# Input turned as landed with its root applied later, gate rows scaled ahead, and both residuals turned by VectorE through shuffled transfers

## The chip, the core and the metric

The kernel runs on one core of one Trainium2 chip. The metric is the device time of one execution in microseconds. The core has five engines with instruction streams of their own that wait for one another on semaphores: TensorE (PE) multiplies, VectorE (DVE) and ScalarE (ACT) work elementwise, GpSimd (POOL) makes masks and issues transfers, and SyncE (SP) issues the weight transfers. Sixteen DMA engines carry every transfer, whichever engine issued it.

## What is computed

One decoder block over 16 meta tokens and 256 tokens, width 2048, all in float32. The reference, cut to what matters here:

```python
h = jnp.concatenate([meta, x], axis=1)              # 272 tokens
u = rmsnorm(h, attn_norm_w[l])                      # x * rsqrt(mean(x*x)) * w
z = u @ w_in[l]
hq, hf, hi, hg, aq, ak, av, iq, ik, iw, ga, gb = split_cols(z, IN_SIZES)
y_h = hgrn2_mix(hq, hf, hi, hg, lbs[l], hgrn_norm_w[l])
y_a = dsa_mix(aq, ak, av, iq, rmsnorm(ik, idx_k_norm_w[l]), iw, topk)
m = (jax.nn.sigmoid(ga) * (y_h @ w_branch_hgrn[l])
     + jax.nn.sigmoid(gb) * (y_a @ w_branch_dsa[l]))
h = h + m @ w_out[l]                                # first residual
u = rmsnorm(h, ffn_norm_w[l])
a = causal_dwconv(u @ w_ffn_gate[l], ffn_conv_w[l], ffn_conv_b[l])
h = h + (jax.nn.silu(a) * (u @ w_ffn_up[l])) @ w_ffn_down[l]   # second residual
return rmsnorm(h, final_norm_w)[:, N_META:]
```

## The kernel before

**Tiling.** Channels lie on the 128 partitions and tokens along the free dimension, so an input of 2048 channels is 16 blocks `k`. The work is cut into units: one unit is 128 output channels. For precision each float32 operand is split in a high and a low part (fp32r), and a unit is 16 steps of three products, high x high, low x high, high x low: 48 products of 128x128 weights with 258 columns (the 256 tokens and two meta tokens), accumulated in one PSUM bank. `u_hi`, `u_lo` hold the normalized input, `w_hi`, `w_lo` the weights of a unit, four buffers each.

**Stages.** 2 key units (done as one), 8 query, 24 recurrence, 32 gate, 24 attention, 8 output-gate, 16 merge, 16 output (`U_OUT`), then twice 44 feed-forward and 22 down units. The recurrence and the attention themselves run as jobs between products.

**Feeding.** SyncE loads weight panels of two units (2 MB) in two slots `raw`, each after `lo_ready` says that the slot's last unit has been split. ScalarE rounds a unit (`w_hi <- raw`, L1057) three units ahead and VectorE makes the rest (`w_lo`, L1358); `ahead(n)` does that for unit n+3. `projected` counts the units TensorE has finished.

**Start.** `x_tok` holds the meta rows and two halves of x with tokens on partitions. ScalarE sums squares (L1104, L1109), VectorE takes the root and scales `x_tok` (L1376, L1390); TensorE then turns three 128x128 pieces for each k (L673), ScalarE rounds them with the norm weight (L1127, `u_hi`), VectorE makes the rest (L1401, `u_lo`), and the key products (L652 to L654) and the first query unit follow. 36 products of ones (`warm_up`, L638) fill TensorE's time until then. After eight steps of unit 3 stands `key_squares` (L686).

**Gates.** The 32 gate units are spilled to DRAM: ScalarE copies the bank to `gate_st` and issues the transfer (L1231). In the merge stage GpSimd fetches a pair of gate rows into one of four buffers (L571) when `m_ready` says that the buffer is free; ScalarE applies the sigmoid (L1283).

**Output stage.** GpSimd fetches x again in panels (`x_st`, L577, L578). TensorE turns three pieces of it into the bank (L952) and accumulates the unit's 48 products on top (L960 to L962); banks 6 and 7 alternate, and unit n waits for `out_free`, the copy of unit n-2. VectorE copies the bank to `h_res` (L1691), ScalarE rounds it (L1296, `u2_hi`, shown as `u_hi`), VectorE makes the rest (L1693), both split a weight unit, GpSimd adds the squares (L583, L588), whose sum over channels TensorE makes within the first feed-forward unit (L979, L981).

**Down stage.** Tokens on partitions. TensorE turns `h_res` back into each bank before its first product (`residual`, L1000, four pieces to a bank, eight banks), and VectorE copies the bank to `h_tok` (L1748) in the first half; in the second half it adds.

The order in every engine is the order of the code; nothing is scheduled by a planner. The loops of the output stage are hardware loops (`Fori`).

## Time and profile before

| | |
|---|---|
| median of 3 runs | 1605.2 us (1605.15 to 1605.24) |
| profiled execution, its own time | 1604.96 us |
| its span | 1603.3 us |
| TensorE busy | 1590.7 us, 99% |
| VectorE busy | 961.1 us, 60% |
| ScalarE busy | 708.9 us, 44% |
| GpSimd busy | 91.9 us, 6% |
| moved by DMA | 290.36 MB, 181 GB/s |

The profile is one execution; times in it are counted from the span's start. In its rows PE is TensorE, DVE VectorE, ACT ScalarE, POOL GpSimd, SP SyncE; a q behind the name is that engine's own sequencer, where transfers are issued. L952 is line 952 of the kernel before. `out<-in` names what is written and read. Matmuls are pipelined, so the duration of one is longer than the distance to the next.

### The profile page before, as it was taken

Reading aid. Unit: us, or ns where it says so; the run is one execution under the profiler, and the core shown is the slowest. Engines: PE = TensorE matmul, PEld = TensorE weight load, DVE = VectorE, ACT = ScalarE, POOL = GpSimd, SP = SyncE. Lnnn points to the kernel's source line nnn. Section 1 sums busy time; section 2 is a strip of 40 time slices with the busy share of each in tenths; the row PEclk is TensorE's granted clock in tenths of the full one; section 3 lists DMA queues with packets and bytes.
Section 4 is the critical chain, followed back from the end, with each engine's and each line's share of the span. In section 5 each row is a group of like instructions: output and inputs, shape, how many; then the busy total and the mean of one; then the engine's idle time right before and its main releaser. Section 6 shows DMA issues by size and latency. Waiting matters only on the chain.

```text
span 1603.3 us, 29430 instructions
## 1 busy us (share of the span) xinstructions
PE 1590.7 (99%) x12222; PEld 1533.2 (96%) x12222; DVE 961.1 (60%) x1117; ACT 708.9 (44%) x741; POOL 91.9 (6%) x149
## 2 busy tenths in 40 slices
PE   9999999999999999999999999999999999999998
PEld 8999999999999999999999999999889999999886
DVE  7555778853355566766566666665445666666453
ACT  6333554544443345754435455544333334334342
POOL 1100050000000001111320000000000000000000
PEclk9999999999999999999999999999999999999999
DMA  7655565555555553577556565645455656565551
GB/s 236 207 158 166 162 200 178 179 178 178 178 162 185 183 158 106 176 231 239 182 170 203 164 198 169 201 165 191 178 206 172 198 171 195 166 200 193 200 209 54
DMA packets 244966, 290.36 MB, mean 181 GB/s; under 512 B 5665, under 2 KB 231186, under 8 KB 244498
## 3 DMA queue, kind: packets, MB, share of 16 engines
q1 hardware_dynamic: 238114, 278.78, 53.4%
q0 software_dynamic: 2176, 6.34, 1.2%
q10 hardware_dynamic: 4608, 4.23, 0.8%
q8 instruction: 55, 0.90, 0.2%
q14 instruction: 13, 0.11, 0.0%
HBM read 283.02 MB, written 6.32 MB: 180 GB/s over the span
## 4 chain that ended last, share of the span: by engine, by line
PE 98%; DVE 1%; ACT 0%; DMA 0%; issue 0%; SPq 0%; DVEq 0%; ACTq 0%
PE ps L616 25%; PE ps L617 24%; PE ps L618 24%; PE ps L1016 5%; PE ps L1015 5%; PE ps L1013 5%; PE ps L962 2%; PE ps L960 2%; PE ps L961 2%; PE ps L738 1%; PE ps L713 0%; PE ps L855 0%; PE ps L952 0%; DMA x_tok<-in_x_dram 0%; PE ps L748 0%; PE ps L1000 0%
## 5 line engine op out<-in xcount | busy, mean ns | idle before, releaser
L616 PE MATMUL ps<-u_hi,w_hi 128*128 128x258 f32 (+2 forms) x2944 | 841.0, 286 | 0.0
L617 PE MATMUL ps<-u_lo,w_hi 128*128 128x258 f32 (+2 forms) x2944 | 833.6, 283 | 0.0
L618 PE MATMUL ps<-u_hi,w_lo 128*128 128x258 f32 (+2 forms) x2944 | 833.2, 283 | 0.0
L1358 DVE TENSOR_TENSOR w_lo<-raw,w_hi 128x2048 fp32r<-128x2048 f32 x259 | 595.6, 2300 | 358.4 <-ACT w_hi L1057 358.1
L1057 ACT ACTIVATE w_hi<-raw 128x2048 fp32r<-128x2048 f32 x259 | 496.1, 1916 | 573.9 <-PE ps L618 411.5
L616 PEld LDWEIGHTS ps<-u_hi,w_hi 128*128 128x128 f32 x2944 | 555.5, 189 | 5.1 <-DVE z_qf L1458 2.5
L617 PEld LDWEIGHTS ps<-u_lo,w_hi 128*128 128x128 f32 x2944 | 555.4, 189 | 0.3
L618 PEld LDWEIGHTS ps<-u_hi,w_lo 128*128 128x128 f32 x2944 | 555.2, 189 | 0.0
L1013 PE MATMUL ps<-w_hi,hid_hi 128*128 128x512 f32 x352 | 137.7, 391 | 0.0
L1016 PE MATMUL ps<-w_lo,hid_hi 128*128 128x512 f32 x352 | 137.0, 389 | 0.0
L1015 PE MATMUL ps<-w_hi,hid_lo 128*128 128x512 f32 x352 | 137.0, 389 | 0.0
L1016 PEld LDWEIGHTS ps<-w_lo,hid_hi 128*128 128x128 f32 x352 | 66.1, 188 | 13.8
L1015 PEld LDWEIGHTS ps<-w_hi,hid_lo 128*128 128x128 f32 x352 | 66.1, 188 | 13.5
L1013 PEld LDWEIGHTS ps<-w_hi,hid_hi 128*128 128x128 f32 x352 | 66.1, 188 | 13.4
L960 PE MATMUL ps<-m_hi,w_hi 128*128 128x258 f32 x256 | 73.7, 288 | 0.0
L962 PE MATMUL ps<-m_hi,w_lo 128*128 128x258 f32 x256 | 72.6, 284 | 0.0
L961 PE MATMUL ps<-m_lo,w_hi 128*128 128x258 f32 x256 | 72.2, 282 | 0.0
L1229 ACT ACTIVATE gate_st<-ps 128x258 f32<-128x258 f32 x32 | 12.4, 387 | 100.0 <-PE ps L618 100.0
L961 PEld LDWEIGHTS ps<-m_lo,w_hi 128*128 128x128 f32 x256 | 48.6, 190 | 0.0
L960 PEld LDWEIGHTS ps<-m_hi,w_hi 128*128 128x128 f32 x256 | 48.4, 189 | 0.0
L962 PEld LDWEIGHTS ps<-m_hi,w_lo 128*128 128x128 f32 x256 | 48.3, 189 | 0.0
L1731 DVE TENSOR_TENSOR g_raw<-ps,h_rs 128x258 f32<-128x258 f32 x44 | 18.8, 427 | 39.6 <-PE ps L618 37.9
(288 smaller groups left out, 1280.0 us busy)
## 6 DMA issues: line engine op xcount, KB each, us to landing
raw<-in_w_in_dram SPq DMA_DIRECT2D x48, 2048.0 KB, 8.4
raw<-in_w_ffn_gate_dram SPq DMA_DIRECT2D x22, 2048.0 KB, 8.0
raw<-in_w_ffn_up_dram SPq DMA_DIRECT2D x22, 2048.0 KB, 8.0
raw<-in_w_ffn_down_dram SPq DMA_DIRECT2D x20, 2048.0 KB, 7.7
raw<-in_w_out_dram SPq DMA_DIRECT2D x8, 2048.0 KB, 8.9
raw<-in_w_branch_hgrn_dram SPq DMA_DIRECT2D x8, 1024.0 KB, 5.4
raw<-in_w_branch_dsa_dram SPq DMA_DIRECT2D x8, 1024.0 KB, 8.5
gate_spill<-gate_st ACTq DMA_DIRECT2D x32, 129.0 KB, 3.8
```

Of the source, the lines that this page charges most:

```text
L616: mm(acc, w_hi[s][:, k, :], mov_hi(k), start=(k == first), stop=False)
L617: mm(acc, w_hi[s][:, k, :], mov_lo(k), start=False, stop=False)
L618: ins = mm(acc, w_lo[s][:, k, :], mov_hi(k), start=False, stop=(k == last))
L960: mm(acc, w_hi[n % 4][:, k, :], m_hi[:, k, :], start=False, stop=False, skip_group_check=True)
L961: mm(acc, w_hi[n % 4][:, k, :], m_lo[:, k, :], start=False, stop=False, skip_group_check=True)
L962: ins = mm(acc, w_lo[n % 4][:, k, :], m_hi[:, k, :], start=False, stop=(k == KT - 1), skip_group_check=True)
L1013: mm(acc, hid_hi[:, f, rows], down_hi[s][:, i, :], start=(f == 0 and half == 1), stop=False, skip_group_check=True)
L1015: mm(acc, hid_lo[:, f, rows], down_hi[s][:, i, :], start=False, stop=False, skip_group_check=True)
L1016: ins = mm(acc, hid_hi[:, f, rows], down_lo[s][:, i, :], start=False, stop=(f == FH - 1), skip_group_check=True)
L1057: activation(w_hi[m % 4][:], raw[(m // 2) % 2][:, :, P * (m % 2):P * (m % 2) + P], ACT.Copy)\
L1358: v.tensor_tensor(w_lo[m % 4][:], raw[(m // 2) % 2][:, :, P * (m % 2):P * (m % 2) + P], w_hi[m % 4][:].bitcast(F32), ALU.subtract).then_in ...
L1731: link(v.tensor_tensor(g[:], ps[4 * half + u][:, 0:TQ], h_rs[:], ALU.mult))
```

## The change

The input: x is turned by TensorE as it lands, without its root. The meta rows come first (16 pieces), then seven blocks of the first 128 tokens, seven more, then the second 128 tokens. `u_hi` and `u_lo` hold x times the norm weight. The roots are computed beside the first units, spread over the partitions by one product of ones with a diagonal (`x_rs`), and every eviction of a unit multiplies by `x_rs`. The gate rows are spilled unscaled; GpSimd multiplies each fetched pair by `x_rs` (`scale_gates`). Warm-up products: 5 where there were 36. The key and first query panels are loaded in halves.

The first residual: GpSimd fetches x in four groups of sixteen transfers (`x_quad`), each 32 partitions x 8 x 32 elements, so that 32x32 blocks lie where a VectorE transpose of blocks gives the full transpose. VectorE turns them (`xt`, and `xm` for the meta rows) and adds them to the bank.

The second residual: VectorE turns each `h_res` by blocks into one of four `h_sh`, ScalarE issues four transfers that write it shuffled to DRAM (`h_spill`), GpSimd loads all of it to `h_tok` after the stage, and VectorE adds the banks to it.

```diff
+        x_blocks = x[0].rearrange("(b j) (k a i) -> a j k b i", j=32, a=4, i=32)
+        meta_blocks = meta_tokens.rearrange("j (k a i) -> a j k i", a=4, i=32)
+        h_blocks = h_spill.rearrange("(b j) (k a i) -> a j k b i", j=32, a=4, i=32)
...
+
+        def x_part(n):
+
+            if n <= EARLY:
+                return n - 1, x_bank(n - 1)[:, 0:P], slice(META, END)
+            if n <= 2 * EARLY:
+                return n - EARLY - 1, x_bank(n - EARLY - 1)[:, 2 * P:3 * P], slice(END, T)
+            return n - EARLY - 1, x_bank(n - EARLY - 1)[:, 0:2 * P], slice(META, T)
...
+            def scale_gates(slot, count):
+                pool.wait_ge(gate_in[slot], count)
+                pool.tensor_tensor(gates[slot][:], gates[slot][:],
+                                   x_rs[:, T0:T].rearrange("p (a t) -> p a t", a=1).to_broadcast([P, 2, TQ]), ALU.mult)\
+                    .then_inc(gate_scaled, 1)
...
+                    scale_gates((a + 3) % 4, 16 * i + (16 if a == 0 else 32))
...
+            def x_quad(q):
+                for a in range(4):
+                    for k in range(4):
+                        pool.dma_start(x_sh[q % 2][32 * a:32 * a + 32, k, :].rearrange("j (b i) -> j b i", i=32),
+                                       x_blocks[a, :, 4 * q + k, :, :]).then_inc(x_sh_in[q % 2], 16)
...
-            for b in range(2):
-                steps.link(pool, pool.memset(x_st[b][:, 0, :], 0.0))
-                x_panel(b, slice(256 * b, 256 * b + 256))
...
+            pool.wait_ge(projected, U_MERGE)
+            pool.wait_ge(ya_ready, 9)
+            pool.memset(xm_sh[:], 0.0).then_inc(xm_zeroed, 1)
+            x_quad(0)
+            pool.wait_ge(xm_zeroed, 1)
+            for a in range(4):
+                pool.dma_start(xm_sh[32 * a:32 * a + 2, :, :], meta_blocks[a, T0:META, :, :]).then_inc(xm_in, 16)
+            pool.wait_ge(projected, U_OUT)
+            x_quad(1)
+            for n in range(16):
+                if n in (4, 8):
+                    pool.wait_ge(xt_turned, n)
+                    x_quad(n // 4 + 1)
...
+            for c in range(2):
+                pool.dma_start(h_tok[c][:], h_spill[:, 1024 * c:1024 * c + 1024].rearrange("(t p) n -> p t n", p=P))\
+                    .then_inc(h_in, 16)
...
-            warm_up(14)
+            warm_up(3)
...
+            def turn(out, t, k):
+                return nc.tensor.transpose(out, x_tok[t][:, P * k:P * k + P], ident[:])
+
+            pe.wait_ge(meta_zeroed, 1)
+            pe.wait_ge(x_in[0], 16)
+            for b in range(4):
+                for k in range(4):
+                    ins = turn(ps[b][:, P * k:P * k + P], 0, 4 * b + k)
+                ins.then_inc(meta_turned, 1)
+            pe.wait_ge(norm_ready, 1)
+            pe.wait_ge(x_in[1], 16)
+            for k in range(EARLY):
+                if k >= 3:
+                    pe.wait_ge(meta_weighted, k - 2)
+                turn(x_bank(k)[:, 0:P], 1, k).then_inc(x_turned, 1)
+            for k in range(EARLY, 2 * EARLY):
+                pe.wait_ge(ul_ready, k - EARLY + 1)
+                turn(x_bank(k)[:, 0:P], 1, k)
+            pe.wait_ge(x_in[2], 16)
+            for k in range(EARLY):
+                turn(x_bank(k)[:, 2 * P:3 * P], 2, k).then_inc(x_turned, 1)
+
...
+            def turn_rest(k):
+
+                pe.wait_ge(ul_ready, k + 1)
+                if k >= 2 * EARLY:
+                    turn(x_bank(k)[:, 0:P], 1, k)
+                turn(x_bank(k)[:, P:2 * P], 2, k).then_inc(x_turned, 1)
...
+            pe.wait_ge(key_hi, 1)
+            for k in range(8):
+                keys_high(k)
+                if k + 11 < KT:
+                    turn_rest(k + 11)
+                if k == 1:
+                    pe.wait_ge(key_lo, 1)
+                    keys_low(0)
+                if k >= 1:
+                    keys_low(k)
+            pe.wait_ge(hi_ready, 2)
+            for k in range(8, KT):
+                keys_high(k)
+            pe.wait_ge(lo_ready, 2)
+            for k in range(8, KT):
...
+            def spread_roots():
+                pe.wait_ge(x_diag, 3)
+                mm(ps[2][:, 0:T], ones[:], diag[:, P - META:3 * P], start=True, stop=True).then_inc(x_spread, 1)
...
-                    bank = ps[6 + u % 2]
-                    for t in range(3):
-                        ins = mm(bank[:, P * t:P * t + P], x_st[u // 2][:, t, P * (u % 2):P * (u % 2) + P], ident[:],
-                                 is_transpose=True, start=(t == 0), stop=False, skip_group_check=True)
-                    ins.then_inc(xt_turned, 1)
...
+                        ins = products(ps[6 + u % 2][:, 0:TQ], n % 4, (k,), lambda k: m_hi[:, k, :],
+                                       lambda k: m_lo[:, k, :])
...
-                        if f == 0 and half == 0:
-                            residual(c, j % 2, t)
...
+            def round_x(n):
+
+                k, part, toks = x_part(n)
+                act.wait_ge(x_turned, n)
+                activation(u_hi[:, k, toks], part, ACT.Copy, scale=vec_a[:, V_ATTN + k:V_ATTN + k + 1])\
+                    .then_inc(uh_ready, 1)
+
+            def round_keys(half):
+
+                activation(w_hi[0][:, half, 0:KEYS], raw[0][:, half, 0:KEYS], ACT.Copy)\
...
+                round_x(n)
+            act.wait_ge(meta_weighted, 4)
+            activation(u_hi[:, :, 0:META], u_meta[:], ACT.Copy).then_inc(meta_rounded, 1)
+            for n in range(EARLY + 1, KT + EARLY + 1):
+                if n == 2 * EARLY:
+                    act.wait_ge(key_in, 16)
+                    round_keys(slice(0, 8))
+                if n == 2 * EARLY + 2:
+                    act.wait_ge(landed[0], landed_by[0])
+                    round_keys(slice(8, KT))
+                if n == KT + EARLY:
+                    act.wait_ge(query_in, 16)
+                    activation(w_hi[2][:, 0:8, :], raw[1][:, 0:8, 0:P], ACT.Copy).then_inc(hi_half, 1)
+                round_x(n)
+            act.wait_ge(landed[1], landed_by[1])
+            activation(w_hi[2][:, 8:KT, :], raw[1][:, 8:KT, 0:P], ACT.Copy).then_inc(hi_ready, 1)
+            round_unit(3, 3, landed_by[1])
+            activation(junk[:], x_tok[1][:], ACT.Square, accum_out=rstat[:, 1:2]).then_inc(x_sum, 1)
             act.wait_ge(x_sum, 3)
-            act.wait_ge(x_part, 2)
-            activation(rstat[:, 5:6], rstat[:, 2:3], ACT.Sqrt, bias=rstat[:, 7:8], scale=1.0 / D).then_inc(x_std, 1)
...
+            for u in range(16):
+                act.wait_ge(out_free, u + 3)
+                activation(u2_hi[:, u, :], h_res[:, u, :], ACT.Copy, scale=vec_a[:, V_FFN + u:V_FFN + u + 1])\
+                    .then_inc(u2h_ready, 1)
+                ahead(U_OUT + u + 1)
+                act.wait_ge(h_turned, u + 1)
+                for a in range(4):
+                    act.dma_start(h_blocks[a, :, u, :, :],
+                                  h_sh[u % 4][32 * a:32 * a + 32, :].rearrange("j (b i) -> j b i", i=32))\
+                        .then_inc(h_out[u % 4], 16)
             act.wait_ge(ssq_sum, 1)
...
+            def rest_x(n):
+
+                k, part, toks = x_part(n)
+                dve.wait_ge(uh_ready, n)
+                v.scalar_tensor_tensor(u_lo[:, k, toks], part, vec_a[:, V_ATTN + k:V_ATTN + k + 1],
+                                       u_hi[:, k, toks].bitcast(F32), ALU.mult, ALU.subtract).then_inc(ul_ready, 1)
+
...
+            dve.wait_ge(x_std, 1)
+            v.reciprocal(rstat[:, 0:3], rstat[:, 3:6]).then_inc(x_rstd, 1)
+            dve.wait_ge(x_rstd, 1)
+            for t in range(3):
+                v.tensor_scalar(diag[:, P * t:P * t + P], ident[:], rstat[:, t:t + 1], None, ALU.mult).then_inc(x_diag, 1)
+            dve.wait_ge(x_spread, 1)
+            v.tensor_copy(x_rs[:], ps[2][:, 0:T]).then_inc(x_rs_ready, 1)
+            dve.wait_ge(x_rs_ready, 1)
             dve.wait_ge(projected, 2)
-            v.tensor_copy(k_raw[0:KEYS, :], ps[1][0:KEYS, 0:T]).then_inc(z_free, 2)
...
-                v.tensor_copy(z_g[:, h, :], ps[m % 2][:, 0:TQ]).then_inc(z_free, 1)
+                v.tensor_tensor(z_g[:, h, :], ps[m % 2][:, 0:TQ], x_rs[:, T0:T], ALU.mult).then_inc(z_free, 1)
...
+            for u in range(16):
+                m, h = U_OUT + u, h_res[:, u, :]
+                if u == 0:
+                    dve.wait_ge(xm_in, 64)
+                    v.transpose(xm[:].rearrange("p k t -> p (k t)"), xm_sh[:].rearrange("p k t -> p (k t)"))\
+                        .then_inc(xm_turned, 1)
+                    dve.wait_ge(xm_turned, 1)
+                if u % 4 == 0:
+                    dve.wait_ge(x_sh_in[(u // 4) % 2], 256 * (u // 8) + 256)
+                v.transpose(xt[u % 2][:], x_sh[(u // 4) % 2][:, u % 4, :]).then_inc(xt_turned, 1)
+                dve.wait_ge(xt_turned, u + 1)
+                dve.wait_ge(projected, m + 1)
+                v.tensor_tensor(h[:, 0:2], ps[6 + u % 2][:, 0:2], xm[:, u, 0:2], ALU.add)
+                v.tensor_tensor(h[:, 2:TQ], ps[6 + u % 2][:, 2:TQ], xt[u % 2][:], ALU.add).then_inc(out_free, 1)
+                dve.wait_ge(u2h_ready, u + 1)
+                v.scalar_tensor_tensor(u2_lo[:, u, :], h, vec_a[:, V_FFN + u:V_FFN + u + 1], u2_hi[:, u, :].bitcast(F32),
+                                       ALU.mult, ALU.subtract).then_inc(u2l_ready, 1)
+                ahead(m + 1, m + 1)
+                if u >= 4:
+                    dve.wait_ge(h_out[u % 4], 64 * (u // 4))
+                v.transpose(h_sh[u % 4][:], h[:, 2:TQ]).then_inc(h_turned, 1)
...
-                    if half == 0:
-                        v.tensor_copy(h, bank).then_inc(down_added, 1)
-                    else:
-                        v.tensor_tensor(h, bank, h, ALU.add).then_inc(down_added, 1)
+                    v.tensor_tensor(h, bank, h, ALU.add).then_inc(down_added, 1)
```

The order of the instructions, at two places. Output stage, ScalarE; before, inside its loop:

```order
L1296 ACTIVATE u_hi<-h_res,vec_a 128x258
L1054 REGISTER_ALU
L1056 ISA
L1057 ACTIVATE w_hi_53<-raw_50 128x2048
L1295 REGISTER_ALU
L1296 ISA x2
L1296 ACTIVATE u_hi<-h_res,vec_a 128x258
L1054 REGISTER_ALU
L1057 ACTIVATE w_hi_54<-raw_50 128x2048
```

and now:

```order
L1391 ACTIVATE u_hi<-h_res,vec_a 128x258
L1142 ACTIVATE w_hi_54<-raw_50 128x2048
L1396 DMA h_spill<-h_sh_134 32x8x32 x4
L1391 ACTIVATE u_hi<-h_res,vec_a 128x258
L1142 ACTIVATE w_hi_51<-raw_49 128x2048
L1396 DMA h_spill<-h_sh_135 32x8x32 x4
```

Between the weights of one unit and the next rounding of h now stand four issues, which wait for VectorE's `h_sh`. The same stage on VectorE (L1691 is the copy, L1693 and L1812 the rest of u2, L1358 and L1455 the rest of a weight unit); before:

```order
L1691 COPY h_res<-ps 128x258
L1692 REGISTER_ALU
L1693 ISA
L1693 SCALAR_TENSOR_TENSOR u_lo<-h_res,vec_a,u_hi 128x258
L1357 REGISTER_ALU
L1358 TENSOR_TENSOR w_lo_57<-raw_50,w_hi_53 128x2048
```

and now:

```order
L1806 STREAM_TRANSPOSE xt_129<-x_sh_128 128x256
L1809 TENSOR_TENSOR h_res<-ps,xm 128x2
L1810 TENSOR_TENSOR h_res<-ps,xt_129 128x256
L1812 SCALAR_TENSOR_TENSOR u_lo<-h_res,vec_a,u_hi 128x258
L1455 TENSOR_TENSOR w_lo_57<-raw_50,w_hi_53 128x2048
L1817 STREAM_TRANSPOSE h_sh_133<-h_res 128x256
```

A block transpose of x stands ahead of the add, and one of h behind the weights. GpSimd, at the passage from merge to output; before:

```order
L591 MEMSET ssq 128x258
L593 MEMSET x_st_124 128x256
L577 DMA x_st_124<-in_x_dram 128x2x256
L578 DMA x_st_124<-in_meta_tokens_dram 2x256
L593 MEMSET x_st_125 128x256
```

and now:

```order
L608 TENSOR_TENSOR gates_125<-gates_125,x_rs 128x516
L645 MEMSET ssq 128x258
L648 MEMSET xm_sh 128x512
L631 DMA x_sh_127<-in_x_dram 32x8x32 x16
L652 DMA xm_sh<-in_meta_tokens_dram 2x16x32 x4
L631 DMA x_sh_128<-in_x_dram 32x8x32 x16
```

The last gate pair is scaled first, and 20 issues stand ahead of the first add where there were two.

## Rows read from the trace of the kernel before

**Rows 1.** The page's first part: busy us, share of the span, instructions.

```profile
PE 1590.7 (99%) x12222; PEld 1533.2 (96%) x12222; DVE 961.1 (60%) x1117; ACT 708.9 (44%) x741; POOL 91.9 (6%) x149
```

**Rows 2.** TensorE's waits: who for whom, total us, times, longest.

```profile
PE ps L616 <- DVE gates L1673: 0.9, 1, 0.9
```

**Rows 3.** Chain in order of time: start us, us, what; output stage, sums, down stage.

```profile
755.73 0.33 PE ps L952 x3
...
767.94 0.33 PE ps L952 x3
...
850.61 0.43 PE ps L981 x2
...
1100.30 0.43 PE ps L1000 x4
```

**Rows 4.** TensorE's timeline in unit 3: start us, us, instruction.

```profile
36.44 0.72 PE L686 MATMUL ps<-k_sq,ones 64*128 64x272 f32 x2
```

**Rows 5.** Timeline of the start: start us, us, instruction, [idle before, releaser].

```profile
1.91 6.17 PE L638 MATMUL ps<-ones 128*128 128x128 f32 x28 [1.91 <-POOL bias L484]
...
6.90 1.92 ACT L1104 ACTIVATE junk<-x_tok 128x2048 f32<-128x2048 f32 x1 [0.27 <-DMA x_tok<-in_x_dram]
...
8.16 4.29 PE L638 MATMUL ps<-ones 128*128 128x128 f32 x36
...
13.62 2.38 ACT L1127 ACTIVATE u_hi<-ps,vec_a 128x272 fp32r<-128x272 f32 x6 [0.26 <-PE ps L673]
```

**Rows 6.** Timelines of VectorE and ScalarE in one output unit, together.

```profile
780.30 0.43 DVE L1691 COPY h_res<-ps 128x258 f32 x1 [0.79 <-PE ps L962]
780.95 0.51 ACT L1296 ACTIVATE u_hi<-h_res,vec_a  x1 [3.77 <-DVE h_res L1691]
781.37 1.90 ACT L1057 ACTIVATE w_hi<-raw 128x2048 fp32r<-128x2048 f32 x1
...
783.30 2.66 DVE L1358 TENSOR_TENSOR w_lo<-raw,w_hi 128x2048 fp32r<-128x2048 f32 x1 [1.18 <-ACT w_hi L1057]
```

**Rows 7.** VectorE's timeline: the key normalization, then a merge unit.

```profile
38.66 1.84 DVE L1431 RECIPROCAL k_rs<-k_rs 128x272 f32<-128x272 f32 x1
...
41.67 0.28 DVE L1436 MEMSET score<- 128x272 f32 x1
...
728.65 2.29 DVE L1358 TENSOR_TENSOR w_lo<-raw,w_hi 128x2048 fp32r<-128x2048 f32 x1 [0.73 <-ACT w_hi L1057]
730.86 0.42 DVE L1681 TENSOR_TENSOR m_lo<-gates,m_hi 128x258 f32 x1
```

**Rows 8.** GpSimd's groups by form: instruction, count, busy us, mean ns.

```profile
L583 POOL TENSOR_TENSOR h_sq<-h_res 128x258 f32 x12 | 7.5, 623 | 19.3 <-DVE h_res L1691 19.2
L577 POOL DMA_DIRECT2D x_st<-in_x_dram x8 | 6.2, 769 | 45.5 <-PE ps L952 44.9 <-POOL x_st L593 0.6
```

**Rows 9.** GpSimd's timeline at the last gate request.

```profile
731.94 0.72 POOL L571 DMA_DIRECT2D gates<-gate_spill  x1 [4.95 <-DVE m_lo L1681]
```

**Rows 10.** ScalarE's timeline in the gate stage.

```profile
388.24 0.34 ACTq L1231 DMA_DIRECT2D gate_spill<-gate_st  x1
388.63 1.92 ACT L1057 ACTIVATE w_hi<-raw 128x2048 fp32r<-128x2048 f32 x1 [0.41 <-ACT gate_st L1229]
```

**Rows 11.** Transfers: KB each, median us from issue to landing (672 to 740, whole).

```profile
gates<-gate_spill POOLq DMA_DIRECT2D x12, 258.0 KB, 5.4
...
x_st<-in_meta_tokens_dram POOLq DMA_DIRECT2D x8, 2.0 KB, 5.9
```

**Rows 12.** Stage row, 745 to 834: PE busy, granted clock, DMA share, GB/s.

```profile
745.00:834.00 89.00, 89.00 (x746) 1.00 0.61 197
```

**Rows 13.** DMA: packets in 9 to 10 us; queue q10 in 300 to 340.

```profile
DMA packets 975, 0.31 MB, mean 312 GB/s; under 512 B 975, under 2 KB 975, under 8 KB 975
...
q10 hardware_dynamic: 864, 0.79, 5.9%
```

**Rows 14.** Stage row, 1.9 to 3 us: busy, clock (third from the end), DMA.

```profile
1.90:3.00 1.10, 1.09 (x5) 1.09 (x6) 1.10 (x1) 1.06 (x1) 0.00 (x0) 1.00 0.72 164
```

More of the change, by code:

```diff
@@ L42 @@
 KEYS = 64 + IDXH
-LEFT = 1280
+EARLY = 7
 U_KI = 0
@@ L1719, in _ @@
                         if u == 3:
+                            if half == 0:
+                                for r in range(4):
+                                    dve.wait_ge(h_out[r], 4 * 64)
                             low(0)
```

315 lines of the change are left out of this document (141 added, 174 removed).

## The prediction

> **What bounds the kernel now.** I read the page first: TensorE is busy for 99% of the span, VectorE for 60, ScalarE for 44 [rows 1]. What TensorE executes is therefore the time, apart from its waits, and the list of its waits holds, beside the wait for the first constants, nothing longer than 0.9 us [rows 2]. A change can gain by taking work from TensorE or by letting its steady run begin earlier, and it loses where it makes a feeding engine slower than TensorE. The averages of VectorE and ScalarE don't tell that, so I then read the timelines of the two stages where the change loads them, the start and the output projection. All sums are in the clock of the profiled execution (span 1603.3, time 1604.96 us); the median of the three runs is 0.24 above it.
>
> **TensorE's pace.** Two output units last 12.21 us (755.73 to 767.94), of which two groups of three transposes are 0.66 [rows 3]. So a unit of 48 products is 5.78 us, 0.12 a product.
>
> **Start: the roots out of the way.** Before, squares, roots and the scaling of x stand between its landing and its transposes. The first product of key_squares stands after eight of the sixteen steps of unit 3, at 36.44 [rows 4]; 24 products earlier, at 33.55, unit 3 began.
> After, x is turned as it lands: tokens 0 to 127 at 6.9 [rows 5], 16 meta transposes before. Then ScalarE sets the pace. Six roundings of 272 columns take 2.38, 0.40 each [rows 5]; 2048 weights take 1.90 [rows 6]. From these I take 0.28 for 128 columns, 0.39 for 256, 0.65 for half the key weights, 1.05 for half a query unit. First turned block at 8.0; seven roundings to 10.0; the meta one to 10.4; TensorE's next transposes let the eighth begin at 10.75; six to 12.4; key weights to 13.1; two to 13.75; key weights to 14.4; seven to 17.15; query weights to 18.2; the last to 18.6; VectorE's rest of it to 19.1. TensorE then has two high products and eight low ones left: 20.3. Unit 2: 16 high products to 22.2, eight low ones to 23.2, a wait until VectorE has made the second half of its low weights (19.1 + 1.2 + 2.2 for a sum of squares over 2048 columns + 1.2 = 23.7), 24 more to 26.6. The product that spreads the roots adds two fp32 records like L686, about 0.65. **Net 33.55 - 26.6 - 0.65 = -6.3 us.** By the same steps units 4 to 7 have their low weights 2 to 4 us before TensorE comes. The evictions become products with x_rs; for 258 columns a copy out of PSUM takes 0.43 and a product of two operands 0.42 [rows 6, 7], so they cost nothing, and the roots lie in VectorE's free time.
> **Gates.** GpSimd scales each pair after it lands: 516 columns, twice an h_sq of 0.62 [rows 8], 1.25 us in a unit of 5.78 in which it had one issue of 0.72 [rows 9]. A pair is asked for four units before it is used and needs some 7 of those 23 us. Nothing, then; uncovered it would be 1.25 a unit, 20 us.
>
> **Transposes that leave TensorE.** The order shows all 48 with x_st and all 32 with h_res gone. 16 x 0.33 = **-5.3 us**, if TensorE isn't made to wait, and 8 groups of four at 0.43 = **-3.5 us** [rows 3]; for the latter VectorE adds where it copied, far ahead of need.
>
> **What the output stage gets instead.** VectorE's row for a unit is: turn x, add (h is made), rest of u2, rest of a weight unit, turn h. ScalarE's is: round u2, round a weight unit, wait until h is turned, issue four transfers, and only then the next unit. That closes a loop: h(u) turned, four issues, u2_hi(u+1), w_hi, w_lo, h(u+1) turned. Its length: hand-over 0.2 (copy ends 780.73, ScalarE starts 780.95); four issues of 0.34 [rows 10] with 0.04 between, 1.5; u2_hi to the start of w_hi 0.42; w_hi 1.90 and hand-over 0.03 [rows 6]; w_lo 2.21 until the next operation starts [rows 7]; and the 32x32 transpose of 256 columns, which this trace doesn't have. Around it stand a memset of 272 columns (0.28), a product of 258 (0.42) and, far off, a reciprocal of 272 (1.84) [rows 7]. I take 0.40, as an operation that passes each column once, and keep 0.28 to 0.6 for the range (at 1.84 the loop would cost 20 us more). Sum **6.66 us against TensorE's 5.78**. Before, ScalarE idled 3.77 us ahead of each u2_hi [rows 6]. Bounds of the loop: 6.35 (hand-over 0.1, issues 1.36, transpose 0.28) and 7.3 (issues 1.7, w_lo 2.6 as beside GpSimd [rows 6], transpose 0.6). add(u) frees the bank of unit u+2, so TensorE can run one unit ahead of it and no more.
> When does the loop start? GpSimd issues x_sh behind the gates. The last gate request is at 731.94 [rows 9] and lands after some 5.4 [rows 11]: 737.3; scaling 1.25 and two memsets: 739.5; 16 issues at 0.78 [rows 8] to 752.0; four shorter ones for the meta rows, which I put at 0.55, the last at 753.6; landing 5.9 later [rows 11]: 759.5. VectorE turns both (0.7 + 0.4) and adds: add(0) ends at A0 = 761.3. Output unit 0 starts at 749.6 (6.1 before the row at 755.73 [rows 3]), so TensorE ends unit 1 at 749.6 + 2 x 5.78 = 761.2 and wants that bank then: the slack is gone at the first unit. A1 = A0 + 6.1, A2 = A0 + 12.8, A15 = A2 + 13 x 6.66 = **860.7**; the square of unit 15 (0.2 + 0.62) and its product (0.1 + 0.43) end at 862.0. Before, that product, L981, ended at 851.04 [rows 3]. The stage is **+11.0 us** longer where it should be 5.3 shorter: the loop costs 16.3. Weights don't run out, since w_lo of unit u+4 is ready 5 us after add(u), two loops before TensorE wants it; after the stage all catch up.
> **Sum:** -6.3 + 11.0 - 3.5 = +1.2; 1606.2 for the profiled execution, **1606.4** by the median.
>
> **Rivals.** (A) *The loop doesn't bind*: the issues run beside ScalarE's activations and x_sh is there in time. Then -6.3 - 5.3 - 3.5 = -15.1: **1590.1**. For it: TensorE's work really goes. Against: in the gate stage the next activation starts at 388.63, after the issue of 388.24 to 388.58, not beside it [rows 10].
> (B) *Short packets fill the DMA engines* (slower). x comes in and h goes out in pieces of 32 elements, 128 bytes: in two units 2048 reads and 2048 writes, 128 of each per engine. In this stage the engines are busy for 0.61 [rows 12], 7.4 of 12.2 us; a double loop of 13.3 leaves 5.9, so it decides from 5900 / 128 = 46 ns for a read and a write together. Key weights of 320 bytes came at 975 packets in 1 us, 16 ns on each of 16 engines; the gate spill's writes took 5.9% of 16 x 40 us for 864 packets, 44 ns [rows 13]. At 16 + 16 it is hidden; at 44 + 44 two units take 7.4 + 11.3 = 18.7 us, 2.7 more per unit, 38 in 14 units, less some 15 us by which the weights run ahead: +23, **1629**. I hold 16 for likelier, since those packets moved 312 GB/s, as fast as long ones.
> The Trainium skill, page DMA: Bandwidth & Descriptors, section Specifications, says that below 512 B an engine reads, modifies and writes. By that rule the writes of h would be the dear half and B likelier; the 320-byte rows of this trace are loads and don't decide it.
> (C) *Slow TensorE at the start.* 28 records of the ones-products took 6.17 us from 1.91, 36 took 4.29 from 8.16 [rows 5]: the first ran at half the rate, though the clock's row there says 1.00 [rows 14]. The change drops 31 of 36 such products. If the low rate lasts to 20 us, 45 key products take 0.12 more each, a part of it covered: about +4.5, **1610.9**.
> The Trainium skill, page TensorE: Matmul & The Clock Gate, Part 1, tells of 1.2 GHz until the array has been busy and 2.4 GHz then; that is C's mechanism.
>
> **How the numbers follow.** Forecast 0.62. Its own range: 14 loops of -0.3 to +0.65 are -4.3 to +9, the landing of x_sh 2 either way, the start 1: 1600 to 1617. A 0.11, B 0.15, C 0.12. A measurement of this kernel tells about 0.2%, 3.2 us. Faster than 1602.0: A and 0.12 of the forecast, 0.23. Within: 0.36 of the forecast and 0.01 of C, 0.37. Slower than 1608.4: B, 0.11 of C, 0.14 of the forecast, 0.40. The range 1600 to 1619 leaves out A and the far end of B, 0.19.
>
> **What would show it.** The last product of unit 2 near 26.6. In the output stage ScalarE's wait ahead of its issues ends with VectorE's h_sh, add(u) comes every 6.6 us, and TensorE waits for VectorE's h_res some 0.9 us a unit, 10 to 16 us in all. If TensorE's waits stay as short as now, A is right; if w_hi waits for a weight transfer, or h_sh for h_spill, B; if products before 20 us come at 0.24 us, C. I would be wrong above all if four issues cost ScalarE far from 1.5 us, or the shuffled transfers land far from 6 us after their issue.

## The result: 4 us slower

The changed kernel takes 1609.53 us, the median of 8 runs (1608.50 to 1612.13), against 1605.24 for the kernel before (1604.99 to 1605.32) on the same chip: ratio 1.0029, 95% interval 1.0019 to 1.0039. That is +4.3 us where +1.2 was forecast. The profiled execution took 1610.17 us (span 1608.6), 5.2 more than that of before. The forecast stands by its mechanism and is off in three sizes, of which one offset a part of the other two; the experiments below take them apart.

The page of the changed kernel, first part; it answers to [rows 1]:

```profile
PE 1581.4 (98%) x12082; PEld 1520.2 (95%) x12082; DVE 977.0 (61%) x1175; ACT 708.5 (44%) x746; POOL 148.0 (9%) x218
```

TensorE lost 9.3 us of work and the kernel became slower: TensorE now waits. Its waits from 740 to 870 us (who for whom, total us, times, longest); before, the longest wait after the start was the one of [rows 2], elsewhere:

```profile
PE ps L679 <- DVE h_res L1810: 11.4, 11, 1.4
PE ps L679 <- DVE u_lo L1812: 3.2, 1, 3.2
PE ps L1075 <- POOL h_sq L637: 0.4, 1, 0.4
```

The timeline of one output unit, VectorE and ScalarE together (start us, us, instruction, [idle before, releaser]); it answers to [rows 6]:

```profile
836.15 0.44 DVE L1817 STREAM_TRANSPOSE h_sh<-h_res 128x256 f32<-128x256 f32 x1
...
836.62 2.02 ACTq L1396 DMA_DIRECT2D h_spill<-h_sh  x4
...
838.70 0.51 ACT L1391 ACTIVATE u_hi<-h_res,vec_a 128x258 fp32r<-128x258 f32 x1 [4.78 <-issue]
839.11 1.90 ACT L1142 ACTIVATE w_hi<-raw 128x2048 fp32r<-128x2048 f32 x1
...
841.04 2.29 DVE L1455 TENSOR_TENSOR w_lo<-raw,w_hi 128x2048 fp32r<-128x2048 f32 x1 [1.32 <-ACT w_hi L1142]
843.25 0.44 DVE L1817 STREAM_TRANSPOSE h_sh<-h_res 128x256 f32<-128x256 f32 x1
```

This is the loop of the forecast, from one turned h to the next in 7.10 us: hand-over and issues 2.55, u2_hi 0.41, w_hi and hand-over 1.93, w_lo 2.21. ScalarE's idle time ahead of u2_hi, once a wait for the copy of h, now is "issue": of the 4.78 us its sequencer waits 2.70 for the turned h and is then busy for 2.02 with the four transfers. The adds of units 1 to 15 start at 759.04 and 858.15 us, 7.08 apart.

The start of the loop: GpSimd's issues, and VectorE's first operations of the stage.

```profile
735.27 9.28 POOL L631 DMA_DIRECT2D x_sh<-in_x_dram  x16
744.54 2.40 POOL L652 DMA_DIRECT2D xm_sh<-in_meta_tokens_dram  x4
...
751.85 0.71 DVE L1801 STREAM_TRANSPOSE xm<-xm_sh 128x512 f32<-128x512 f32 x1 [2.95 <-DMA xm_sh<-in_meta_tokens_dram]
752.60 0.45 DVE L1806 STREAM_TRANSPOSE xt<-x_sh 128x256 f32<-128x256 f32 x1
753.08 0.16 DVE L1809 TENSOR_TENSOR h_res<-ps,xm 128x2 f32<-128x2 f32 x1
753.16 0.41 DVE L1810 TENSOR_TENSOR h_res<-ps,xt 128x256 f32<-128x256 f32 x1
```

The first part of the kernel: TensorE's first transposes, ScalarE's first roundings, and the first scores, a landmark that both kernels have.

```profile
4.49 4.53 PE L710 MATMUL ps<-ident,x_tok 128*128 128x128 f32 x23 [0.72 <-DMA x_tok<-in_meta_tokens_dram]
...
8.45 1.92 ACT L1195 ACTIVATE u_hi<-ps,vec_a 128x128 fp32r<-128x128 f32 x7 [1.99 <-PE ps L710]
...
69.81 0.97 PE L817 MATMUL ps<-ki,iq_st 64*128 64x144 f32 x8
```

In the kernel before, the same scores (L713 there) stand at:

```profile
75.21 0.97 PE L713 MATMUL ps<-ki,iq_st 64*128 64x144 f32 x8
```

So the start gained 5.4 us, not 6.3. From here the account is simple: 5.4 us ahead, the product with h_sq (L1075) ends at 860.02 us against 851.04 before, 9.0 us behind, so the output stage cost 14.4; the end is 5.2 behind, so the down stage gave 3.8 back.

### The profile page after: what moved, and what is told of

Same layout as the page of the kernel before. It is cut to its first block, busy times and chain, and to the rows that moved or that the text cites. A ratio compares the mean times of both kernels' runs of the same rounds, so it can differ in the third digit from the quotient of the medians.

```text
span 1608.6 us, 29146 instructions
## 1 busy us (share of the span) xinstructions
PE 1581.4 (98%) x12082; PEld 1520.2 (95%) x12082; DVE 977.0 (61%) x1175; ACT 708.5 (44%) x746; POOL 148.0 (9%) x218
## 3 DMA queue, kind: packets, MB, share of 16 engines
q0 software_dynamic: 4000, 8.45, 1.9%
## 4 chain that ended last, share of the span: by engine, by line
PE 90%; issue 3%; ACT 2%; ACTq 2%; DVE 1%; POOL 1%; DMA 1%; SPq 0%; DVEq 0%; POOLq 0%
PE ps L679 24%; PE ps L680 23%; PE ps L681 23%; PE ps L1101 5%; PE ps L1098 5%; PE ps L1100 5%; ACT w_hi L1142 2%; ACTq L1396 2%; PE ps L842 1%; POOL x_sh L631 1%; PE ps L817 0%; DVE h_sh L1817 0%; PE ps L710 0%; PE ps L959 0%; DMA xm_sh<-in_meta_tokens_dram 0%
## 5 line engine op out<-in xcount | busy, mean ns | idle before, releaser
L1455 DVE TENSOR_TENSOR w_lo<-raw,w_hi 128x2048 fp32r<-128x2048 f32 x259 | 597.2, 2306 | 352.4 <-ACT w_hi L1142 352.0
L1098 PE MATMUL ps<-w_hi,hid_hi 128*128 128x512 f32 x352 | 136.9, 389 | 0.0
L679 PE MATMUL ps<-m_hi,w_hi 128*128 128x258 f32 x256 | 73.4, 287 | 11.4 <-DVE h_res L1810 11.4
L1098 PEld LDWEIGHTS ps<-w_hi,hid_hi 128*128 128x128 f32 x352 | 66.1, 188 | 13.6
L1391 ACT ACTIVATE u_hi<-h_res,vec_a 128x258 fp32r<-128x258 f32 x16 | 8.2, 512 | 78.9 <-issue 71.9
```

What stands on the lines that cost most here:

```text
L679: mm(acc, w_hi[s][:, k, :], mov_hi(k), start=(k == first), stop=False)
L1098: mm(acc, hid_hi[:, f, rows], down_hi[s][:, i, :], start=(f == 0), stop=False, skip_group_check=True)
L1455: v.tensor_tensor(w_lo[m % 4][:], raw[(m // 2) % 2][:, :, P * (m % 2):P * (m % 2) + P], w_hi[m % 4][:].bitcast(F32), ALU.subtract).then_in ...
```

## The experiments

All times are medians; every kernel was timed beside the kernel before, which took 1605.3 to 1605.4 us each time. Each is given as an edit to the changed kernel.

| kernel | us | against before |
| --- | --- | --- |
| start and gates alone | 1599.97 | 0.9967 (0.9954 to 0.9979) |
| and x turned by VectorE | 1594.13 | 0.9930 (0.9917 to 0.9944) |
| the change | 1609.53 | 1.0029 (1.0019 to 1.0039) |
| h turned ahead of w_lo | 1590.27 | 0.9905 (0.9890 to 0.9921) |
| issues behind the next rounding | 1594.09 | 0.9929 (0.9915 to 0.9942) |
| that, last two behind the root | 1594.47 | 0.9927 (0.9913 to 0.9941) |
| that of two rows up, x early | 1590.44 | 0.9907 (0.9892 to 0.9922) |
| the change, x early | 1608.17 | 1.0017 (1.0008 to 1.0026) |
| the change, eight issues | 1637.41 | 1.0198 (1.0182 to 1.0213) |
| h ahead of w_lo, ten warm-ups | 1591.55 | 0.9913 (0.9900 to 0.9927) |
| h ahead of w_lo, one warm-up | 1589.99 | 0.9903 (0.9888 to 0.9918) |
| that, x early | 1589.90 | 0.9904 (0.9887 to 0.9922) |

**The parts one by one.** First the start and the gates alone, with the output and down stages of before:

```
-                products(..., m_hi, m_lo)                # output unit without x
+                transpose(x_st) x3, products onto them   # as before
-                v.transpose(xt), two adds; v.transpose(h_sh); four issues; load of h_tok
+                v.tensor_copy(h, bank); residual(c, u, t) on TensorE, as before
```

> The change's first two parts alone: the new start and the gates scaled by GpSimd. The output stage and the down stage are those of before (x_st and h_res turned by TensorE, no transfers of h). Theory (the start gains what the trace of the changed kernel shows at L817, 75.28 - 69.88 = 5.4 us, nothing of it is lost before the end, and the gates cost nothing): 1605.2 - 5.4 = 1599.8 us, the output stage as long as before. Rival (part of the stage's +14.4 us comes from the first parts, for instance from weight loads that run at another distance, or the gates): 1602 us or more. The forecast's start term, -6.3, would give 1598.9.

It took 1599.97 us: -5.4. Its trace is 5.5 us ahead at the first scores (69.69 us) and 5.3 at the product with h_sq (845.16 against 850.44), so the gates cost some 0.2 us at most, and none of the first parts lengthens the output stage.

Then x turned by VectorE as in the change, but h turned by TensorE:

```
-                v.transpose(h_sh[u % 4][:], h[:, 2:TQ])
-                act.wait_ge(h_turned, u + 1); four act.dma_start(h_blocks..., h_sh...)
-            pool.dma_start(h_tok[c][:], h_spill...)
+                residual(c, j % 2, t)                    # in the down stage, as before
```

> The changed kernel with the first residual turned by VectorE, but the second by TensorE as before: no turned copy of h, no issues of its transfers on ScalarE, no load of h. Theory (the output stage was stretched by the loop through ScalarE's four issues; without them no loop is over TensorE's 5.78 us): the stage is TensorE's again and shorter than before by the 5.3 us of x_st, so 1605.2 - 5.4 (start) - 5.3 = 1594.5 us. Rival 1 (the turn of x and the two adds, with their transfers, stretch the stage by themselves): over 1600 us. Rival 2 (the late first add, which waits for the input's transfers, costs): 1596 to 1599 us.

1594.13 us, the first theory's 1594.5: taking x's transposes away is worth 5.8 us, and the turn of x, its two adds and the shuffled loads cost nothing. Whatever cost 15 us and more in the change stands in the lines taken out here.

**The loop, broken in two places.** The first kernel moves one operation of VectorE:

```
                 v.scalar_tensor_tensor(u2_lo[:, u, :], ...)
+                if u >= 4:
+                    dve.wait_ge(h_out[u % 4], 64 * (u // 4))
+                v.transpose(h_sh[u % 4][:], h[:, 2:TQ]).then_inc(h_turned, 1)
                 ahead(m + 1, m + 1)                      # w_lo
-                (the same three lines)
```

> The changed kernel with one step of VectorE moved: h(u) is turned ahead of the rests w_lo instead of behind them, all work and all transfers the same. Theory (the loop: ScalarE's issues wait for h turned, that waits for w_lo, that for w_hi, and the next u2_hi waits behind the issues): with the turn ahead of w_lo ScalarE has 0.42 + 1.93 + about 1.9 = 4.3 us of work a unit, under TensorE's 5.78; the output stage falls from 7.11 to 5.8 us a unit, about 20 us: 1589 to 1591 us. Rival 1 (the transfers of 128 bytes stretch the stage, by the DMA engines' time): 1603 to 1610, no better than the changed kernel. Rival 2 (ScalarE's issues take their time from its sequencer, whatever the order): about 1600.

1590.27 us: 19.3 us less than the change, with every instruction and every transfer kept. This is what the loop cost. Both rivals fall with it: transfers of 128 bytes and issues on ScalarE are all there, in a shorter stage. ScalarE's timeline in one unit of this kernel shows why:

```profile
826.10 1.90 ACT L1142 ACTIVATE w_hi<-raw 128x2048 fp32r<-128x2048 f32 x1
827.10 1.82 ACTq L1396 DMA_DIRECT2D h_spill<-h_sh  x4
831.25 0.51 ACT L1391 ACTIVATE u_hi<-h_res,vec_a 128x258 fp32r<-128x258 f32 x1 [3.24 <-DVE h_res L1810]
```

The issues still wait for the turned h, but that no longer waits for w_lo: VectorE has it at 827.07 us, so they begin beside the activation, 1.0 us into it, and end 2.3 us before the next u2_hi may start. Stage rows of 820 to 840 us (length, then busy us of PE, PEld, DVE, ACT, POOL, granted clock, DMA share, GB/s), first the change, then this kernel:

```profile
820.00:840.00 20.00, 16.81 (x136) 16.19 (x135) 11.47 (x18) 5.94 (x6) 3.79 (x6) 1.00 0.52 158
```

```profile
820.00:840.00 20.00, 20.00 (x166) 19.89 (x165) 13.56 (x22) 9.27 (x8) 4.86 (x8) 1.00 0.78 232
```

The second kernel leaves VectorE's order and moves ScalarE's issues:

```
                 ahead(U_OUT + u + 1)                     # w_hi
-                act.wait_ge(h_turned, u + 1); four issues for h(u)
+                if u:
+                    store_h(u - 1)                       # the same wait and four issues
+            store_h(15)
```

> The changed kernel with ScalarE's four issues for h(u) put behind the rounding of unit u + 1 (u2_hi and w_hi) instead of unit u; VectorE's order is that of the changed kernel. Theory (the same loop, broken at its other end: the turned h is there when its issues' turn comes): as with the turn ahead of the rests, 1589 to 1591 us, within 1 us of it. Rival (the transfers or the issues themselves cost): 1600 to 1610 us.

1594.09 us: better than the change by 15.4, but 3.8 worse than the first. The loop through the issues is gone, and VectorE's timeline shows another behind it:

```profile
830.75 0.41 DVE L1816 TENSOR_TENSOR h_res<-ps,xt 128x256 f32<-128x256 f32 x1
831.75 0.49 DVE L1818 SCALAR_TENSOR_TENSOR u_lo<-h_res,vec_a,u_hi 128x258 fp32r<-128x258 f32 x1 [0.58 <-ACT u_hi L1399]
833.56 2.29 DVE L1461 TENSOR_TENSOR w_lo<-raw,w_hi 128x2048 fp32r<-128x2048 f32 x1 [1.32 <-ACT w_hi L1142]
835.77 0.44 DVE L1823 STREAM_TRANSPOSE h_sh<-h_res 128x256 f32<-128x256 f32 x1
836.13 0.40 DVE L1812 STREAM_TRANSPOSE xt<-x_sh 128x256 f32<-128x256 f32 x1
836.57 0.16 DVE L1815 TENSOR_TENSOR h_res<-ps,xm 128x2 f32<-128x2 f32 x1
836.64 0.41 DVE L1816 TENSOR_TENSOR h_res<-ps,xt 128x256 f32<-128x256 f32 x1
```

From add to add 5.89 us, with no wait for TensorE in it: add, u2_hi, w_hi, w_lo, both turns, add. It is only 0.1 us slower than TensorE's 5.78 [rows 3], but a loop that is slower never catches up, so the first add's lateness (754.02 us; 752.05 in the other kernel, whose loop is 5.56 since h is turned beside ScalarE's rounding) is carried to the end and grows by 0.1 us a unit: the last add starts at 842.52 us instead of 836.52. My own reading of this trace was another one, that the root h_rs, behind six issues (4.6 us of "issue"), held up the feed-forward. So the last two sets went behind the root:

```
             for u in range(16): ...
-                if u: store_h(u - 1)
-            store_h(15)
+                if u and u < 15: store_h(u - 1)
             act.wait_ge(ssq_sum, 1)
             activation(h_rs[:], ps[4][:, 0:TQ], ACT.Sqrt, ...)
+            store_h(14)
+            store_h(15)
```

> The kernel with ScalarE's issues for h(u) behind the rounding of the next unit, and its last two sets of issues, h(14) and h(15), behind the root h_rs instead of ahead of it. It asks where the 3.8 us went by which that kernel is slower than the one with h turned ahead of the rests. Theory (1.5 us of it are a second loop without issues, add 0.5, u2_hi 0.42, w_hi 1.90, w_lo 2.21, turn of h 0.36, turn of x 0.44 = 5.88 us a unit against TensorE's 5.78; the other 2.3 us are the root that waits 4.6 us behind the last six issues): 1591.8 us (1591.3 to 1592.3). Rival (the loss is all in the loop and in the clock that falls behind it): 1594 us, no change.

1594.47 us: no gain. The root did come 5.5 us earlier (845.72 instead of 851.21 us), and nobody was waiting for it; 4.6 us of idle time in a timeline were worth nothing. In both kernels the list has TensorE wait 1.9 us at L1075 for the last h_sq and 0.9 for u2_lo; then it ran slowly. TensorE's stage rows of the kernel with the issues behind the next rounding:

```profile
840.00:844.00 4.00, 2.11 (x15) 1.69 (x14) 3.39 (x6) 1.03 (x2) 0.62 (x1) 1.00 1.11 329
844.00:848.00 4.00, 4.00 (x24) 3.96 (x22) 2.65 (x3) 1.29 (x1) 0.00 (x0) 0.64 0.19 33
848.00:852.00 4.00, 4.00 (x33) 4.00 (x33) 0.28 (x1) 2.06 (x3) 0.00 (x0) 0.93 0.83 251
```

Behind the stretch in which it stood half idle, the granted clock is 0.64, a mixture of 1.2 and 2.4 GHz, and TensorE did 24 and 33 products in 4 us where 36 is full: 15 x 0.12 = 1.8 us. The landmarks of the two kernels agree: L1075 starts at 843.7 us instead of 839.5, 4.2 behind, and the down stage (L1098) at 1095.0 instead of 1089.2, 5.8 behind, so waits cost 4.2 and the clock 1.6. The list shows only 2.8 of the 4.2: product by product, TensorE falls another 1.2 us behind between 780 and 837 us, some 0.12 a unit, in waits too short for the list. It had met the loop of 5.885 there and follows it. The 5.8 are the whole difference of the two profiled executions (1596.03 and 1590.22); the medians differ by 3.8, since the runs of this kernel lie far apart (1592.98 to 1596.03). The Trainium skill, page TensorE: Matmul & The Clock Gate, Part 1, says that an idle array goes back to 1.2 GHz; this trace agrees in kind, behind a stretch in which the array was idle for a part only, and here the slow products added 1.6 us to 4.2 of waits.

**The first add.** Is it its lateness that the loops hand on? GpSimd's transfers of x_sh[0] and xm_sh were moved ahead of the gate loop, in two kernels:

```
             for n in range(3):
                 scale_gates(n, 16)
+            pool.memset(xm_sh[:], 0.0); x_quad(0); four issues for xm_sh
             with pool.Fori(0, 3) as i:                   # gate requests and scalings
-            (behind the loop: the same lines)
```

> The kernel with the issues for h(u) behind the next unit's rounding, and the same early transfers of x_sh[0] and xm_sh. In the kernel without the early transfers the adds came every 5.885 us from 754.02 us on, never nearer to TensorE's pace, so its loss of 3.8 us against the kernel with h turned first would be the late start (752.05 us there) carried to the end by a second loop through w_lo, the turns of h and x and the add. Theory: the first add at 750.1, the last at 750.1 + 15 x 5.885 = 838.4 us instead of 842.5, 1.9 us behind the other kernel's 836.5; since a last add 6.0 us late gave TensorE 2.8 us of waits, 1.9 us are hidden by the first half of the feed-forward's first unit: 1590.3 to 1591 us. Rival (the issues' place itself costs the 3.8 us): 1594 us, no change.

1590.44 us, as expected. The first add starts at 750.16 us, as soon as TensorE is done, and the last, one loop of 5.885 after the other, at:

```profile
838.44 0.41 DVE L1816 TENSOR_TENSOR h_res<-ps,xt 128x256 f32<-128x256 f32 x1
```

That is 1.9 us later than with h turned first, and the trace lists no wait of TensorE between 740 and 870 us. The spread says the same. Without the early transfers the kernel's runs lay between 1592.98 and 1596.03, with them between 1590.33 and 1590.50. The reading that fits is that the loop passed on whatever the landings differed by from run to run; xm_sh's end of landing, the start of its turn, was 750.75, 751.85 and 752.72 us in three profiled executions.

> The changed kernel with one move on GpSimd: the transfers of x_sh[0] and of the last two meta rows, xm_sh, are issued ahead of the gate loop instead of behind it; the loop over ScalarE's issues is left as it is. It asks what the late first add is worth, the term A0 of the prediction. Theory (the loop of 7.1 us starts with the first add, which in the changed kernel began at 753.16 us behind xm_sh's landing; with the rows there, it can begin at the end of unit 0's products, 750.1 us, and a loop that binds hands the 3.0 us on to the end): 1609.5 - 3.0 = 1606.5 us. Rival (the loop's start does not matter, or the gates, whose requests now stand behind 11.7 us of issues, come too late in units 3 and 4 of the merge): 1609.5 us or more.

1608.17 us in the change's own order: 1.4 us gained, not 3.0. The first add started 3.4 us earlier (749.80), the last only 2.2 (855.92), because the first four issues, 1.85 us in the change, took 2.91 here:

```profile
755.28 2.91 ACTq L1396 DMA_DIRECT2D h_spill<-h_sh  x4
```

The direction is that of the theory; why those issues took longer stays open. Of the 2.2 us another 0.6 went to the clock: L1075 started at 857.70 us, 1.6 earlier than in the change (859.32). TensorE's stage rows of this kernel:

```profile
848.00:852.00 4.00, 0.67 (x4) 0.49 (x4) 1.56 (x5) 1.51 (x2) 1.44 (x3) 0.84 0.71 216
852.00:856.00 4.00, 4.00 (x20) 4.00 (x20) 3.14 (x5) 0.80 (x1) 0.00 (x0) 0.50 1.06 342
```

Behind its wait for u2_lo TensorE did 24 products from 851.66 to 856.96 us, 5.3 us where full rate is 2.9. In the change they took 4.5, and h_sq came later still (859.26); here it was there at 857.03 and TensorE came last. In the order that no loop binds, the early transfers should be worth nothing:

> Three edits together on the changed kernel: h turned ahead of the rests, x_sh[0] and xm_sh asked for ahead of the gate loop, one more warm-up product. It is meant as the best version, and asks whether the early transfers are worth anything where no loop binds. Theory (with h turned ahead of the rests TensorE has no idle time in the output stage, 20.00 us busy of each 20, so a first add 2 to 3 us earlier changes nothing, and only the warm-up's 0.3 us count): 1590.0 us (1589.5 to 1590.5), the same as without the early transfers. Rival (a late first add costs there too, as it did in the two other orders): 1587 to 1588.5 us.

1589.90 us against 1589.99 without them: nothing, as expected. Its adds come 5.76 us apart, TensorE's own pace. It is the lowest time of all, by less than the runs differ.

**The issues' price.** Each of the four transfers was cut in two, with the same 1024 pieces of 128 bytes a unit:

```
                 for a in range(4):
-                    act.dma_start(h_blocks[a, :, u, :, :], h_sh[...])
+                    for b in range(0, 8, 4):
+                        act.dma_start(h_blocks[a, :, u, b:b + 4, :], h_sh[..., 32 * b:32 * b + 128])
```

> The changed kernel, in its own order, with each of ScalarE's four transfers of h(u) cut into two of half the size: eight issues a unit with as many pieces of 128 bytes in all. It asks what the issue's price goes by, and whether the loop follows it one to one. Theory (the price is per issue, median 0.47 us): 1.9 us more a unit in the loop, 15 times, +28 us: 1638 us. If an issue costs not less than the 0.31 us that was the shortest: 8 x 0.31 = 2.5 us instead of 1.9, +9 us: 1618 us. Rival (the price is per piece of 128 bytes, so that an issue of half the pieces costs half): 1609.5 us, as the changed kernel. In each case the period of the loop must be 5.2 us and the eight issues' time, and the end must move by 15 times what the period does.

1637.41 us, +27.9: the theory of a price per issue gave 1638. The groups of the two lines, first of the change, then of this kernel (issues, ns min/median/max):

```profile
L1396 ACTq DMA_DIRECT2D h_spill<-h_sh x64: 309/474/1067, 758.6 to 866.6; - x64
```

```profile
L1397 ACTq DMA_DIRECT2D h_spill<-h_sh x128: 309/454/731, 758.4 to 896.5; - x128
```

Half the pieces, the same price. And the loop follows the time of the issues one to one:

```profile
807.41 0.51 ACT L1391 ACTIVATE u_hi<-h_res,vec_a 128x258 fp32r<-128x258 f32 x1 [6.84 <-issue]
...
812.44 3.70 ACTq L1397 DMA_DIRECT2D h_spill<-h_sh  x8
816.19 0.51 ACT L1391 ACTIVATE u_hi<-h_res,vec_a 128x258 fp32r<-128x258 f32 x1 [6.46 <-issue]
```

816.19 - 807.41 = 8.78 us, of which 3.70 issues and 5.08 the rest; in the change 838.70 to 845.59 are 6.89, of which 1.81 and 5.08. On average over the units a set of issues takes 3.93 and 1.98 us, and the adds are 9.00 and 7.08 apart.

**The start.** Did TensorE's slow first transposes cost what the start lacks?

```
             nc.tensor.transpose(ps[6][:, 0:KT], vec_rows[...]...)
+            warm_up(10)
```

> The kernel with h turned ahead of the rests, and ten more warm-up products of 128 x 128 behind the transpose of the norm's rows, in the idle time before the input lands. It asks whether the start lost 0.9 us against the forecast because TensorE turned the first blocks slowly: 23 transposes took 4.53 us, 0.197 us each, where 36 took 4.29 us, 0.119 us each, in the kernel before. Theory (the first rounding waits for these transposes, 8.34 us, and ScalarE paces all that follows, so a faster TensorE brings forward the first rounding only): 0.3 to 1.3 us faster, 1589.0 to 1590.0 us. Rival C as it was priced in the prediction (a slow TensorE costs 4.5 us of the start): 1585.8 us. Rival (the products push the first transposes back, or the pace is ScalarE's in any case): 1590.3 or up to 0.5 us more.

1591.55 us, 1.3 slower than without. I had counted ten products as 2 us; each is two records of 0.21, and they were in the way:

```profile
3.69 4.35 PE L701 MATMUL ps<-ones 128*128 128x128 f32 x20
7.88 2.67 PE L711 MATMUL ps<-ident,x_tok 128*128 128x128 f32 x23
```

The 23 transposes took 2.67 us instead of 5.15 in the same kernel without them, 2.5 less, but began 3.5 later. The first rounding waits for the 17th, the first piece of x behind 16 of the meta rows, and moved from 8.34 to 10.00 us. With one product (warm_up(1) in place of warm_up(10)), which fits into the idle time:

> The kernel with h turned ahead of the rests and one more warm-up product (two records of 0.21 us) behind the norm's transpose, where ten (4.35 us) pushed the first transposes of the input from 4.38 to 7.88 us and cost 1.3 us. Theory (one product ends before the input lands, at 4.38 us, closes TensorE's idle time, and brings the change of its clock from 8.9 us to at best 7.7, which shortens three to six transposes from 0.21 to 0.12 us): 0.3 to 0.5 us faster than without, 1589.8 to 1590.0 us. Rival (nothing that a measurement shows): 1590.3 us.

1589.99 us (1589.47 to 1590.11) against 1590.27 (1589.78 to 1590.32): 0.3 less, the size expected, but the two spreads overlap. Its trace has the first rounding at 8.22 us instead of 8.34: the records shorten at 7.7 us (9.3 without the product), but of the 17 transposes that the first rounding waits for only the last two came behind that.

## Why the prediction was right, and its sizes off

**Start, -6.3; it was -5.4.** The steps held: unit 3 began at 26.84 us where 26.6 was forecast. The first block was turned at 8.45 us and not at 8.0, since the first 17 transposes took 0.21 us each, and the keys ended at 21.3 and not at 20.3. But ScalarE had caught up by its last rounding (18.7 us against 18.6), and the wait for the low weights of unit 2, forecast to 23.7 (they came at 23.69), took up most of what TensorE was late. The product that spreads the roots took 0.46 us (0.65 in the sum). What the sum left out are three transposes, those of the norm vectors. Before, they stood ahead of unit 2 and so within the 33.55; now they stand within unit 3, behind the 26.6 (the kernel before, then the changed kernel):

```profile
27.20 0.51 PE L680 MATMUL ps<-ident,vec_rows 94*128 94x94 f32 x3
```

```profile
30.88 0.51 PE L774 MATMUL ps<-ident,vec_rows 94*128 94x94 f32 x3
```

They put off the next products by 0.54 us. So +0.24, -0.19 and +0.54; another 0.3 us up to the first scores I can't assign. The landmark at 69.81 and the medians of the kernel with the start alone both give 5.4. Rival C's mechanism is real, but its price is within the 0.24: the slow records end at 8.1 us in the change's trace and at 9.3 in that of the kernel with h turned first, where they fall from 418 to 273 ns, and not at 20.

**Gates, nothing.** Right: GpSimd's scaling took 1.49 us on average (1.25 forecast) and TensorE's one wait for the gates is still 0.9 us, as in [rows 2].

**Transposes, -5.3 and -3.5.** Right in kind and slightly low: from kernel to kernel 5.8 us for those of x (1599.97 to 1594.13) and 3.9 for those of h (1594.13 to 1590.27).

**The loop, 6.66; it was 7.08.** The mechanism, its members and TensorE's waits (10 to 16 us in all; 11.4 in 11 waits) are as forecast. Of its terms the transpose is 0.44 (0.40 taken; a reciprocal's 1.84, the far bound, was no neighbour), and all but the issues come to 5.08 (5.16). The mis-sized term is the issues': 2.0 us for four, not 1.5. I took 0.34 from an issue with 128 rows in the gate stage [rows 10], a single row of an idle queue; the median here is 0.47. 14 distances between adds 1 and 15 make that +5.8 us against the sum.

**The loop's start, A0.** The first add ended at 753.57 us, 758.97 in the clock of before (5.4 added), not at 761.3: 2.3 us sooner. GpSimd's issue of x_sh takes 0.58 us, not the 0.77 on average that [rows 8] show for x_st (0.78 in the sum), so 16 took 9.28 us instead of 12.5; they began 1.2 us later than forecast (735.27, which is 740.67 in the clock of before, against 739.5). The landing time held, 5.9. The early-transfer kernels show that the term belongs in the sum.

**The stage: +11.0; it was +14.4.** -2.3 (A0), -0.2 (A1), +5.8 (the adds) and +0.1 (the last square) make +3.4. Altogether the profiled execution is +0.9 (start), +3.4 and -0.3 (down stage) away from the forecast's +1.2, which gives +5.2. It was luck that these offset one another: with the right A0 the forecast would have been 2.3 us lower, a small gain over the kernel before, and missed by over 5.

**Rival A** (the loop doesn't bind, 1590.1) is what the kernel becomes when one line moves: 1590.27. (Its sum, -6.3 - 5.3 - 3.5, is the measured -5.4 - 5.8 - 3.9 by chance.) The row that I held against it, an activation that starts only after an issue, tells nothing of the case that matters, an issue beside the activation ahead of it. **Rival B** (short packets) is refuted. Queue q10, which carries h, from 756 to 866 us in the change (packets, MB, share of 16 engines):

```profile
q10 hardware_dynamic: 16320, 1.97, 11.7%
```

0.117 x 16 x 110 us for 16320 packets are 12.6 ns each, where B needed 46 ns for a read and a write. GpSimd's queue, with 33 of x's transfers, took 4.7% of the same stretch, 9.8 ns for each of their 33 x 256 pieces, so both together are 22. A write of 128 bytes was no dearer than a read of 320 in [rows 13]. The Trainium skill, page DMA: Bandwidth & Descriptors, section Specifications, has writes below 512 B read and modify first; if they do, nothing of it shows in these packets' time.

## What to carry to other kernels

An engine that both computes and issues transfers is a link between two others: put behind each other what waits for whom across one unit, count the issues at 0.5 us each, and compare the loop's length with the pace of the engine that sets the time. If the loop is longer, look for the one operation whose place closes it, since moving it costs nothing and here was worth 19 us; and check the loop that is left, since one 0.1 us too long still carries every late start to the end. Taking work from the busiest engine pays only as far as the feeding engines stay under its new pace.
